# A hybrid streaming encoder step with 32 experts: the half pass put last, the overflow loop two passes earlier, two weight units beside the ring, and the gate/up bias loaded within the first pass

## The chip, the cores and the metric

The kernel runs on one core of a Trainium2 chip. The metric is the device time of one execution in microseconds. The profiler's span is the time from the first to the last instruction of the profiled execution; it is a little shorter than the execution's own time.

## The reference, cut to what matters

The layer has a mixer (one wide projection, a gated recurrent branch, a spatial gating branch, an output projection), and behind it a mixture of experts. There are 384 tokens (256 of a prompt, 8 x 16 of running streams), a model width of 1024, 32 experts and 4 experts for each token. All is float32.

```python
x = x + mixer(rms_norm(x, norm1_g), ...)
h = rms_norm(x, norm2_g)
logits = h @ w_router + b_router
gates = softmax(top_k(logits, 4))
for e in range(32):
    gate, up = split(h[tokens_of(e)] @ w_gate_up[e] + b_gate_up[e])    # 1024 -> 2 x 1024
    gate, up = minimum(gate, 7), clip(up, -7, 7)
    act = (up + 1) * gate * sigmoid(1.702 * gate)
    x[tokens_of(e)] += gates_of(e) * (act @ w_down[e] + b_down[e])
y = rms_norm(x, final_norm_g)
```

The weights of one expert are 12 MB (8 MB gate/up, 4 MB down), so the 32 experts bring 384 MB through the DMA.

## The kernel before, in words

**Engines.** The kernel is written with one instruction stream for each engine and semaphores between them. SP (SyncE) issues nearly all loads, in one order written out by hand. POOL (GpSimd) issues a few small loads and prepares for each pass the matrix `pick`, which gathers tokens, and `sel`, which selects bias rows. TensorE (PE) multiplies, ACT and DVE (ScalarE and VectorE) read PSUM.

**The mixer** comes first (to about 294 us of the span). Its weights pass through a small ring of their own (`raw`), are split into a high and a low part by ACT and DVE (L571, L784), and are multiplied at L1208 to L1210. While it runs, places in SBUF come free one after the other, and SP loads the first units of expert weights into them (`load_expert`, L335 to L337 and its calls up to L377).

**Passes.** The experts are ranked by their number of tokens, and 17 passes (`UNITS`, L70) take them in turn. A pair pass takes two experts, each with 64 of the 128 token slots (the two wide passes split 96 and 32). One solo pass (pass 8) gives all slots to one expert. The half pass takes one expert with 64 tokens and puts the two halves of the output columns side by side, so it needs half the matmuls. Before, the order is: passes 0 to 7 pairs and wide pairs, pass 8 solo, 9 to 13 pairs, pass 14 the half pass, 15 and 16 pairs. Passes are counted from 0 here, so "the fifteenth" is pass 14.

**Within a pass** (`experts_pass`, L1503) TensorE does, for k = 0 to 7, the gate/up product of 128 rows of the weights (L1537); behind k=0 it adds the bias by a matmul with `sel` (L1552; the half pass has L1549 and L1550); behind k=1 and k=3 it combines the output of the pass before into PSUM for the three token tiles (L1470, L1471; in pass 0 it is the down bias, L1477), and DVE adds these to y (L1132). Then come the gather of the tokens of the next pass (L1453), the turning of the activations (L1500), for which DVE and ACT have made gate and up (L1146 to L1150, L722), and the down product (L1591). The output is scaled by ACT (L738, in the last pass L735).

**The ring.** Expert weights stand in 16 places of 1 MB (`RING_AT`, `wexp`), and two places together take 2 MB in one load from pass 1 on (L391). One unit is 1 MB; a pair pass needs 24, a solo or half pass 12. The load of unit n waits until TensorE has used unit n - 16 (`wexp_used`). In front of the last pass stands the overflow loop: if an expert had more tokens than its slots, passes are added at run time, in up to three groups of eight. With these inputs no group is taken, but every engine steps over the loop. The first 12 units of the pass behind it wait for unit n - 12, since their places are those which the loop would use.

**Behind the last pass** TensorE combines (L1617, L1618), DVE adds (L1190), ACT squares (L762), DVE and ACT make the roots (L1194 to L1196, L765), and the final gain is applied to token tiles 0 and 2 by DVE (L1200) and to tile 1 by POOL and ACT (L561, L768). SP stores three tiles of 512 KB (L416).

**Bias and gain.** `bias_raw` (0.5 MB) is loaded by POOL in the mixer (L479) and split into its high and low part by DVE at L971 and L972; `fnb`, the final gain in all partitions (0.5 MB written), is loaded by POOL at L475.

Of the kernel before, what the change touches and what calls it, by code (L numbers as in the profile page):

```python
# [34 lines left out]
P = 128  # L35
# [40 lines left out]
OVER_SLOTS = tuple((LOADS[LAST] + m_) % RINGS for m_ in range(EXP_U))  # L76
OVER_ROWS = 5
OVER_GROUP = 8
# [22 lines left out]
def hawk_gmlp_moe_streaming_step(  # L101
# [6 lines left out]
    with ExitStack() as ctx:  # L108
# [4 lines left out]
        def sem(name):  # L113
# [57 lines left out]
        bias_raw = at("bias_raw", 176128, [2 * NE, 2 * D])  # L171
# [5 lines left out]
        fnb = at("fnb", 205824, [P, D])  # L177
# [26 lines left out]
        mask = at("mask", 112128, [P, TT, NE], BF16)  # L204
        iota_p = at("iota_p", 98432, [P, P])
        gat_t = at("gat_t", 201728, [3 * NE, T], F32R)
        gat3 = at("gat3", 203264, [P, TT, 3, NE])
        cnt = at("cnt", 204416, [P, NE])
        key = at("key", 204544, [P, NE])
        rank = at("rank", 204672, [P, NE])  # L210
        cap = at("cap", 204928, [P, 3, NE])
        order_f = at("order_f", 204800, [1, NE])
# [6 lines left out]
        squares = at("squares", 201728, [P, D])  # L219
        y_gain = at("y_gain", 131072, [P, D])  # L220
# [13 lines left out]
        fnb_loaded, n2p_loaded = sem("fnb_loaded"), sem("n2p_loaded")  # L234
# [29 lines left out]
        gat_ready = sem("gat_ready")  # L264
# [16 lines left out]
        sq3, gained, r3_in, r3_out, out_final, stored = (  # L281
            sem("sq3"), sem("gained"), sem("r3_in"), sem("r3_out"), [sem(f"out_final{t}") for t in range(TT)], sem("stored"))
# [45 lines left out]
        def _(sp):  # L328
# [28 lines left out]
            sp.wait_ge(mrg_ready, CB)  # L357
            load_expert(4)
# [20 lines left out]
            for n in range(RINGS, 2 * EXP_U):  # L379
                sp.wait_ge(wexp_used, n - RINGS + 1)  # L380
                sp.dma_start(wexp[n % RINGS][:], exp_one(n % 2, n // 2)).then_inc(exp_landed[n % RINGS], 16)
            sp.wait_ge(order_ready, 1)
            def load_pass(unit, later, ids, ring, last=False):

                for n in range(0, EXP_U * len(ids), 2):
                    m, x, slot = n // 2 // len(ids), n // 2 % len(ids), (unit + n) % RINGS
# [9 lines left out]

            for it in range(1, LAST):
                load_pass(LOADS[it], 0, ranked(it), lambda n: RINGS)
            sp.wait_ge(table_ready, 1)
            groups_on = sp.value_load(cnt_i[0:1, 0:1], min_val=0, max_val=OVER_GROUPS)  # L400
            with sp.Fori(0, OVER_GROUPS) as a:
                with sp.If(a < groups_on):
                    for b in range(OVER_GROUP):
                        e = sp.value_load(over_e[0:1, bass.ds(a * OVER_GROUP + b, 1)], min_val=0, max_val=NE - 1)
                        load_pass(LOADS[LAST], a * (OVER_GROUP * EXP_U) + b * EXP_U, [e], lambda n: EXP_U)
                sp.nop()
            ids = ranked(LAST)
            load_pass(LOADS[LAST], groups_on * (OVER_GROUP * EXP_U), ids, lambda n: EXP_U if n < EXP_U else RINGS, True)
            for k in range(2):
                for x in range(2):  # L410
                    sp.dma_start(wexp[(LOADS[NU] - 3 + 2 * x) % RINGS][:, D * k:D * k + D],
                                 exp_two(ids[x], EXP_U // 2 - 1)[:, D * (2 + k):D * (3 + k)]).then_inc(last_landed[k][x], 16)
            for t, dst in ((0, y_prompt[:, 0:P, :].rearrange("o p d -> (o p) d")), (1, y_prompt[:, P:2 * P, :].rearrange("o p d -> (o p) d")),
                           (2, y_sample.rearrange("b s d -> (b s) d"))):
# [1232 lines left out]
```

## Time and profile before

| | us |
|---|---|
| median of 3 runs | 1244.13 (1243.86 to 1244.79) |
| the profiled execution's own time | 1245.88 |
| its span | 1243.8 |
| TensorE busy | 1181.9 |
| DVE busy | 396.3 |
| ACT busy | 226.7 |
| POOL busy | 82.4 |

The mean granted clock of TensorE is 0.988 of full speed. The DMA moved 443.67 MB in the span. In a window's row the columns are the stretch, its length, busy time and number of instructions of each engine, the granted clock of TensorE as a share of full speed, the busy share of the DMA engines, and GB/s. In a row of the timeline or of the chain the first number is the start in us from the span's start and the second the time in us.

### The profile page before, as it was taken

The numbers are of one execution on the slowest core, as the hardware profiler recorded it, in microseconds if no ns is written. First come the engines' busy times: TensorE is split into PE (matmuls) and PEld (weight loads), VectorE is DVE, ScalarE is ACT, GpSimd is POOL, SyncE is SP. The second block draws the span as 40 slices with busy tenths as digits, with TensorE's granted clock in tenths as the row PEclk, the third lists the DMA queues.
The fourth block names the chain that finished last, engine by engine and source line by source line (L and its number), as shares of the span: only waits on it lengthen the run. The fifth ranks groups of instructions, "written<-read, shape, count | busy, mean of one in ns | idle before, by whom it ended". The sixth has DMA issues, their size and how long they took to land.

```text
span 1243.8 us, 15675 instructions
## 1 busy us (share of the span) xinstructions
PE 1181.9 (95%) x6447; PEld 675.1 (54%) x6447; DVE 396.3 (32%) x649; ACT 226.7 (18%) x389; POOL 82.4 (7%) x243
## 2 busy tenths in 40 slices
PE   7999999999999999989999999999999898999896
PEld 6999999985435354343434343544435353544332
DVE  4648586756242313131211111221211121212023
ACT  4533672223101011010101010100101010110112
POOL 4100000010201010000100010101101010110000
PEclk9999999999999999999999999999999999999898
DMA  6553227578999999999999999899999999999992
GB/s 226 155 166 107 98 86 256 194 291 341 419 428 427 427 428 428 426 426 427 427 428 427 429 426 427 353 385 421 427 428 428 428 427 427 427 428 428 425 422 95
DMA packets 48828, 443.67 MB, mean 357 GB/s; under 512 B 4620, under 2 KB 4716, under 8 KB 22576
## 3 DMA queue, kind: packets, MB, share of 16 engines
q1 hardware_dynamic: 47488, 439.43, 85.6%
q0 software_dynamic: 1264, 3.20, 1.0%
q8 instruction: 51, 0.84, 0.3%
q14 instruction: 25, 0.20, 0.0%
HBM read 440.63 MB, written 1.98 MB: 356 GB/s over the span
## 4 chain that ended last, share of the span: by engine, by line
PE 75%; DMA 21%; issue 1%; DVE 1%; ACT 1%; SPq 1%; DVEq 0%; ACTq 0%
PE ps L1537 24%; DMA wexp<-in_w_gate_up_dram 20%; PE ps L1591 17%; PE ps L1208 7%; PE ps L1453 7%; PE ps L1209 7%; PE ps L1210 7%; PE ps L1470 1%; PE ps L1500 1%; PE ps L1471 1%; PE ps L1308 1%; PE ps L1552 1%; PE ps L1462 1%; DMA raw<-in_w_in_dram 1%; PE ps L1422 0%
## 5 line engine op out<-in xcount | busy, mean ns | idle before, releaser
L1537 PE MATMUL ps<-wexp,xt 128*64 128x512 f32 (+1 forms) x2368 | 479.1, 606 | 34.4 <-DMA wexp<-in_w_gate_up_dram 28.8
L1537 PEld LDWEIGHTS ps<-wexp,xt 128*64 128x64 f32 (+1 forms) x2368 | 155.0, 133 | 328.9 <-issue 328.4
L1591 PE MATMUL ps<-wexp,act_t 128*64 128x512 f32 (+1 forms) x1184 | 232.0, 596 | 4.8 <-issue 4.0
L1591 PEld LDWEIGHTS ps<-wexp,act_t 128*64 128x64 f32 (+1 forms) x1184 | 88.3, 132 | 135.2 <-issue 134.1
L1132 DVE TENSOR_TENSOR y<-y,ps 128x1024 f32<-128x1024 f32 x51 | 60.7, 1218 | 216.9 <-PE ps L1471 214.8
L722 ACT ACTIVATE g<-g 128x512 f32<-128x512 f32 x33 | 20.8, 630 | 567.9 <-DVE g L1146 567.9
L1208 PE MATMUL ps<-act_h,split 128*128 128x384 f32 x352 | 118.0, 335 | 0.0
L1210 PE MATMUL ps<-act_h,split 128*128 128x384 f32 x352 | 117.6, 334 | 0.0
L1209 PE MATMUL ps<-act_l,split 128*128 128x384 f32 x352 | 117.6, 334 | 0.0
L1453 PEld LDWEIGHTS ps<-pick,xn 128*128 128x128 f32 x768 | 86.9, 192 | 13.0 <-issue 13.0
L1170 DVE SCALAR_TENSOR_TENSOR out_l<-ps,gate_now,out_h 128x1024 fp32r<-128x1024 f32 x16 | 20.5, 1283 | 225.4 <-ACT out_h L738 225.4
L1453 PE MATMUL ps<-pick,xn 128*128 128x128 f32 x768 | 90.0, 277 | 0.0
L784 DVE TENSOR_TENSOR split<-raw,split 128x2048 fp32r<-128x2048 f32 x29 | 66.2, 2290 | 69.7 <-ACT split L571 69.6
L1146 DVE TENSOR_SCALAR g<-ps 128x512 f32<-128x512 f32 x33 | 22.7, 687 | 194.7 <-PE ps L1537 194.7
L571 ACT ACTIVATE split<-raw 128x2048 fp32r<-128x2048 f32 x30 | 57.6, 1919 | 95.5 <-PE ps L1210 69.0
L1208 PEld LDWEIGHTS ps<-act_h,split 128*128 128x128 f32 x352 | 66.1, 188 | 0.6 <-issue 0.4
L1209 PEld LDWEIGHTS ps<-act_l,split 128*128 128x128 f32 x352 | 66.1, 188 | 0.1
L1210 PEld LDWEIGHTS ps<-act_h,split 128*128 128x128 f32 x352 | 66.1, 188 | 0.0
L738 ACT ACTIVATE out_h<-ps,gate_now 128x1024 fp32r<-128x1024 f32 x16 | 17.8, 1113 | 212.2 <-PE ps L1591 212.2
L1470 PE MATMUL ps<-out_h,pick_tg 128*128 128x512 f32 x96 | 41.3, 430 | 0.0
L715 ACT ACTIVATE xt<-ps,small 128x128 f32<-128x128 f32 x128 | 36.4, 371 | 18.6 <-PE ps L1453 18.6
L499 POOL TENSOR_SCALAR pick<-iota_p,pos_e 128x64 f32<-128x64 f32 (+2 forms) x93 | 39.2, 445 | 3.3 <-POOL pos_e L512 2.9
(304 smaller groups left out, 814.9 us busy)
## 6 DMA issues: line engine op xcount, KB each, us to landing
wexp<-in_w_gate_up_dram SPq DMA_DIRECT2D x120, 2048.0 KB, 24.0
wexp<-in_w_down_dram SPq DMA_DIRECT2D x58, 2048.0 KB, 25.4
raw<-in_w_in_dram SPq DMA_DIRECT2D x20, 1024.0 KB, 5.1
wexp<-in_w_gate_up_dram SPq DMA_DIRECT2D x16, 1024.0 KB, 8.6
wexp<-in_w_down_dram SPq DMA_DIRECT2D x10, 1024.0 KB, 8.2
raw<-in_w_proj_a_dram SPq DMA_DIRECT2D x4, 1024.0 KB, 5.7
raw<-in_w_out_dram SPq DMA_DIRECT2D x4, 1024.0 KB, 5.0
raw<-in_w_proj_b_dram SPq DMA_DIRECT2D x2, 1024.0 KB, 6.8
```

Source lines behind the costliest of these rows:

```text
L499: i_ = pool.tensor_scalar(pick[:, t, s0:s0 + width], iota_p[:, 0:width], pos_e[:, t, x:x + 1], None, ALU.is_equal)
L571: act.activation(split_h[:, n % MIX_SPLIT], raw[:, n % MIX_RING], ACT.Copy).then_inc(high_done, 1)
L715: i_ = act.activation(xt[:, 4 * k + c, :], ps[:, 4 + k, c * P:(c + 1) * P], ACT.Copy, scale=n2p[:, 4 * k + c:4 * k + c + 1])
L784: dve.tensor_tensor(split_l[:, n % MIX_SPLIT], raw[:, n % MIX_RING], split_h[:, n % MIX_SPLIT].bitcast(F32), ALU.subtract).then_inc(low_do ...
L1132: dve.tensor_tensor(y[:, t, :], y[:, t, :], ps[:, b:b + 2, :].rearrange("p a b -> p (a b)"), ALU.add).then_inc(y_added, 1)
L1208: pe.matmul(out, a_h, b_h, start=start, stop=False)
L1209: pe.matmul(out, a_h, b_l, start=False, stop=False)
L1210: return pe.matmul(out, a_l, b_h, start=False, stop=stop)
L1453: i_ = pe.matmul(ps[:, 4 + c // 4, c % 4 * P:(c % 4 + 1) * P], xn2[:, t, c * P:(c + 1) * P], pick[:, t], start=t == 0, stop=t == TT - 1)
L1470: pe.matmul(o, pick_tg[:, t * P:(t + 1) * P], out_h[:, UC * k:UC * k + UC], start=True, stop=False)
L1537: i_ = pe.matmul(ps[s0:s0 + w, b, :], xt[:, k, s0:s0 + w], wexp[place(k, x)][:, at_:at_ + UC], start=k == 0, stop=k == CB - 1)
L1591: i_ = pe.matmul(ps[s0:s0 + w, 6 + c, :], act_, wexp[place(CB + m, x)][:, D * kk + UC * c:D * kk + UC * c + UC], start=k == 0, stop=k == C ...
```

## The change

- The half pass moves from place 14 to the end; passes 9 to 15 are seven pair passes. In the last pass there is no gather for a next one.
- The overflow loop stands in front of pass 14 (`OVER_AT`), on all engines. Passes 14, 15 and 16 follow it, with their waits counted from a register value.
- Units 0 and 1 (k=0 of the two experts of pass 0) get places of their own, `wfirst`: one in the place of the recurrent branch's weights, loaded by SP within the mixer, one in the place of the low part of the mixer's activations, loaded in front of `load_expert(4)`. The ring's first 16 units are now 2 to 17. A unit still waits for unit n - 16.
- `bias_raw` is loaded by POOL when k=0 of pass 0 is done, into the place of `wfirst[0]`; DVE splits it behind the ranking, in front of its first additions to y; TensorE adds the bias of pass 0 behind k=5 instead of k=0.
- `fnb` is loaded by POOL behind its preparation of pass 2.
- Behind the last pass the token tiles are taken in another order, DVE applies the gain to all three, POOL and ACT to none, and the last tile is stored in two halves.
- Several small tables lie elsewhere in SBUF.

```diff
-         + [((SOLO_RANK,), SOLO)] + [(r, PAIR) for r in PAIR_RANKS[5:10]] + [((HALF_RANK,), HALF)] + [(r, PAIR) for r in PAIR_RANKS[10:12]])
+         + [((SOLO_RANK,), SOLO)] + [(r, PAIR) for r in PAIR_RANKS[5:12]] + [((HALF_RANK,), HALF)])
+OVER_AT = LAST - 2
+PLACES = [n_ - 2 for n_ in LOADS]
+LAST_ORDER = ((0, 0), (1, 0), (0, 1), (1, 1), (2, 0), (2, 1))
...
+        wfirst = [at("wfirst0", 201728, [P, 2 * D]), at("wfirst1", 114688, [P, 2 * D])]
...
             def load_expert(n):
-                sp.dma_start(wexp[n][:], exp_one(n % 2, n // 2)).then_inc(exp_landed[n], 16)
+                u = n + 2
+                sp.dma_start(wexp[n][:], exp_one(u % 2, u // 2)).then_inc(exp_landed[n], 16)
...
+                if n == PB_U + 1:
+                    sp.wait_ge(gates_mm, 4)
+                    sp.dma_start(wfirst[0][:], exp_one(0, 0)).then_inc(first_landed[0], 16)
...
             sp.wait_ge(mrg_ready, CB)
+            sp.dma_start(wfirst[1][:], exp_one(1, 0)).then_inc(first_landed[1], 16)
             load_expert(4)
...
-            for n in range(RINGS, 2 * EXP_U):
-                sp.wait_ge(wexp_used, n - RINGS + 1)
+            for n in range(RINGS, 2 * EXP_U - 2):
+                u = n + 2
+                sp.wait_ge(wexp_used, u - RINGS + 1)
...
-            load_pass(LOADS[LAST], groups_on * (OVER_GROUP * EXP_U), ids, lambda n: EXP_U if n < EXP_U else RINGS, True)
+            load_pass(LOADS[OVER_AT], later, ranked(OVER_AT), lambda n: EXP_U if n < EXP_U else RINGS)
+            for it in range(OVER_AT + 1, LAST):
+                load_pass(LOADS[it], later, ranked(it), lambda n: RINGS)
+            load_pass(LOADS[LAST], later, ids, lambda n: RINGS, True)
...
-            pool.wait_ge(gates_mm, 4)
-            pool.dma_start(fnb[:], final_norm_g...).then_inc(fnb_loaded, 16)
-            pool.wait_ge(unit_used, PA_U)
-            for k in range(2):
-                pool.dma_start(bias_raw[k * NE:(k + 1) * NE, :], ...).then_inc(bias_loaded, 16)
...
+            pool.wait_ge(wexp_used, 2)
+            for k in range(2):
+                pool.dma_start(bias_raw[k * NE:(k + 1) * NE, :], ...).then_inc(bias_loaded, 16)
             pool.wait_ge(order_ready, 1)
-            for it in range(1, LAST):
+            for it in range(1, OVER_AT):
                 prepare(it, it)
+                if it == 2:
+                    pool.wait_ge(combined, TT)
+                    pool.dma_start(fnb[:], final_norm_g...).then_inc(fnb_loaded, 16)
...
-            pool.tensor_tensor(y_gain[:], y[:, 1, :], fnb[:], ALU.mult).then_inc(gained, 1)
...
             dve.tensor_copy(order_i[:], order_f[:]).then_inc(order_ready, 1)
+            dve.wait_ge(bias_loaded, 32)
+            link(dve.tensor_copy(bias_hl[:], bias_raw[:]))
+            dve.tensor_tensor(bias_hl[NE:2 * NE, :], ..., ALU.subtract).then_inc(bias_ready, 1)
...
+            last_stats(slice(0, 2), 4)
             dve.wait_ge(fnb_loaded, 16)
+            gain(0, slice(0, D), 1)
+            last_stats(slice(2, 3), 6)
+            gain(1, slice(0, D), 1)
+            for c in range(2):
+                gain(2, slice(UC * c, UC * c + UC), 2)
...
-                    if k == 0:
+                    if k == (5 if first else 0):
+                        if first:
+                            pe.wait_ge(bias_ready, 1)
                         pe.wait_ge(sel_ready, it + 1)
...
-            experts_pass(groups_on * OVER_GROUP + LAST, LOADS[LAST], groups_on * OVER_GROUP, ..., False, True)
+            for it in range(OVER_AT, NU):
+                experts_pass(groups_on * OVER_GROUP + it, PLACES[it], groups_on * OVER_GROUP, ..., False, it == LAST)
```

## Rows read from the trace of the kernel before

**Rows 1.** The page, part 2: GB/s in 40 equal slices of the span.
```profile
GB/s 226 155 166 107 98 86 256 194 291 341 419 428 427 427 428 428 426 426 427 427 428 427 429 426 427 353 385 421 427 428 428 428 427 427 427 428 428 425 422 95
```

**Rows 2.** The waits, whole span: us in total, times, longest us.
```profile
PE ps L1537 <- DMA wexp<-in_w_gate_up_dram: 28.8, 16, 3.1
...
PE ps L1537 <- issue: 5.3, 1, 5.3
```

**Rows 3.** The chain of work that ended last, in order of time.
```profile
718.12 8.79 PE ps L1537 x32
...
734.25 13.95 PE ps L1591 x64
748.21 3.43 PE ps L1537 x16
...
801.74 3.43 PE ps L1537 x16
...
1050.75 7.09 PE ps L1537 x32
...
1139.78 7.10 PE ps L1537 x32
...
1173.42 6.64 PE ps L1537 x16
```

**Rows 4.** Windows: end of the mixer, and the start of pass 16.
```profile
272.00:281.00 9.00, 9.00 (x49) 6.57 (x47) 1.87 (x5) 2.62 (x7) 0.00 (x0) 1.00 0.04 15
...
1173.40:1180.00 6.60, 6.58 (x17) 1.90 (x17) 0.00 (x0) 0.00 (x0) 0.00 (x0) 0.54 1.01 423
```

**Rows 5.** Timeline of the half pass (pass 14), then of pass 16 and the output.
```profile
1078.93 1.92 PE L1537 MATMUL ps<-wexp,xt 128*64 128x512 f32 x8
...
1097.57 5.62 PE L1453 MATMUL ps<-pick,xn 128*128 128x128 f32 x48
...
1104.60 7.03 PE L1591 MATMUL ps<-wexp,act_t 128*64 128x512 f32 x32
...
1194.90 13.95 PE L1537 MATMUL ps<-wexp,xt 128*64 128x512 f32 x64
...
1213.02 15.65 PE L1591 MATMUL ps<-wexp,act_t 128*64 128x512 f32 x64 [0.83 <-ACT act_t L728]
1227.92 1.48 ACT L735 ACTIVATE out_h<-ps,gate_now 128x512 fp32r<-128x512 f32 x2 [15.41 <-PE ps L1591]
...
1234.35 1.67 DVE L1194 TENSOR_TENSOR small<-small 128x2 f32<-128x2 f32 x1 [0.26 <-ACT squares L762]
...
1236.78 2.48 DVE L1200 SCALAR_TENSOR_TENSOR y<-y,small,fnb 128x1024 f32<-128x1024 f32 x2
```

**Rows 6.** DMA of unit 15, issued by SP (L337) at 286.9 us.
```profile
DMA to landing us min/median/max: 14.5/14.5/14.5
```

**Rows 7.** DMA of unit 18, issued by SP (L381) at 304.1 us.
```profile
DMA to landing us min/median/max: 5.0/5.0/5.0
```

**Rows 8.** Timeline of pass 0: bias, down bias, first additions to y.
```profile
298.19 1.19 PE L1552 MATMUL ps<-bias_hl,sel 64*128 64x512 f32 x4
...
308.59 2.35 DVE L1132 TENSOR_TENSOR y<-y,ps 128x1024 f32<-128x1024 f32 x2
...
312.17 0.73 PE L1477 MATMUL ps<-bdn_hl,gat_t 96*128 96x512 f32 x2
```

**Rows 9.** The tile bias_raw: its conversion on DVE, its loads by POOL.
```profile
L971 DVE CAST bias_hl<-bias_raw x1: 1214/1214/1214, 259.5 to 259.5; 64x2048 fp32r<-64x2048 f32 x1
L972 DVE TENSOR_TENSOR bias_hl<-bias_raw,bias_hl x1: 2281/2281/2281, 260.8 to 260.8; 32x2048 fp32r<-32x2048 f32 x1
...
DMA to landing us min/median/max: 4.8/5.2/5.5
```

**Rows 10.** DMA of unit 32, issued by SP (L391) at 338.0 us.
```profile
DMA to landing us min/median/max: 10.1/10.1/10.1
```

**Rows 11.** Window at the end of the stores.
```profile
1242.50:1243.00 0.50, 0.00 (x0) 0.00 (x0) 0.00 (x0) 0.00 (x0) 0.00 (x0) 0.50 0.67 254
```

More of the change, by code:

```diff
@@ L746, in _ @@
             act.preload_act_table(ACT.Silu)
-            for it in range(LAST):
-                experts_pass(it, LOADS[it], len(UNITS[it][0]), False, UNITS[it][1] is HALF)
+            for it in range(OVER_AT):
+                experts_pass(it, LOADS[it], len(UNITS[it][0]), False)
             act.wait_ge(table_ready, 1)
@@ L761, in _ @@
                     act.wait_ge(sq3, n - 1)
-                act.activation(squares3[:, n % 2], y[:, t, UC * c:UC * c + UC], ACT.Square, accum_out=rt[:, 32 + n:33 + n]).then_inc(sq3, 1)
-            for ts in (slice(0, 2), slice(2, 3)):
-                act.wait_ge(r3_in, 1 if ts.start == 0 else 2)
-                act.activation(rt[:, 40 + ts.start:40 + ts.stop], rt[:, 44 + ts.start:44 + ts.stop], ACT.Sqrt).then_inc(r3_out, 1)
-            act.wait_ge(gained, 1)
-            act.wait_ge(r3_out, 1)
-            act.activation(y_gain[:], y_gain[:], ACT.Copy, scale=rt[:, 41:42]).then_inc(out_final[1], 1)
+                act.activation(squares3[:, n % 2], y[:, t, UC * c:UC * c + UC], ACT.Square,
+                               accum_out=rt[:, 32 + TT * c + t:33 + TT * c + t]).then_inc(sq3, 1)
+                if n == 4:
+                    act.wait_ge(r3_in, 1)
+                    act.activation(rt[:, 40:42], rt[:, 44:46], ACT.Sqrt).then_inc(r3_out, 1)
+            act.wait_ge(r3_in, 2)
+            act.activation(rt[:, 42:43], rt[:, 46:47], ACT.Sqrt).then_inc(r3_out, 1)
         @block.vector
@@ L1513, in landed @@
                     for x in range(experts):
[L1514 removed]
+                        if first and k == 0:
+                            pe.wait_ge(first_landed[x], 16)
+                            continue
+                        slot, turn_ = place(k, x), (unit + 2 * (experts * (k // 2) + x)) // RINGS + 1
                         if first:
[L1516 to L1518 removed]
+                            turn_ = (experts * k + x - 2) // RINGS + 1
                         pe.wait_ge(exp_landed[slot], later * 16 + 16 * turn_ if later is not None and slot in OVER_SLOTS else 16 * turn_)
@@ L1536, in experts_pass @@
                             at_ = UC * (b + n) if half else UC * b
-                            i_ = pe.matmul(ps[s0:s0 + w, b, :], xt[:, k, s0:s0 + w],
-                                           wexp[place(k, x)][:, at_:at_ + UC], start=k == 0, stop=k == CB - 1)
+                            weights = wfirst[x] if first and k == 0 else wexp[place(k, x)]
+                            i_ = pe.matmul(ps[s0:s0 + w, b, :], xt[:, k, s0:s0 + w], weights[:, at_:at_ + UC], start=k == 0, stop=k == CB - 1)
                             if k == CB - 1 and b == 2 and (n == 0 if half else n == len(strips(shape)) - 1):
@@ L1553, in experts_pass @@
                         i_.then_inc(sel_used, 1)
-                        if first:
-                            token_gates(0, 7)
-                            pe.wait_ge(gat3_ready, 1)
-                            for t in range(TT):
-                                i_ = pe.transpose(ps[0:3 * NE, 6, t * P:(t + 1) * P], gat3[:, t].rearrange("p k e -> p (k e)"), ident[:])
-                            i_.then_inc(post_mm, 1)
+                    if first and k == 0:
+                        token_gates(0, 7)
+                        pe.wait_ge(gat3_ready, 1)
+                        for t in range(TT):
+                            i_ = pe.transpose(ps[0:3 * NE, 6, t * P:(t + 1) * P], gat3[:, t].rearrange("p k e -> p (k e)"), ident[:])
+                        i_.then_inc(post_mm, 1)
                     if k == 1:
```

140 lines of the change are left out of this document (68 added, 72 removed).

## The prediction

> **What bounds the kernel now.** I read the page's slices first. From the twelfth slice to the last but one the DMA moves 421 to 429 GB/s, but for two slices after pass 8 (353 and 385) [rows 1], so the expert passes run on a saturated stream of weights, while TensorE is busy too. The waits say how the two share the bound: TensorE waited for gate/up weights 16 times, 28.8 us in all and never over 3.1 us [rows 2]. I call the six steps of a pass A (k=0,1), B (k=2,3), C (k=4,5), D (k=6,7), E and F (the two halves of the down product). The longest waits stand before D. In the chain [rows 3] pass 8 begins at 748.21 and pass 9 at 801.74: 53.53 us for a pass without a wait. From D of pass 13 (1050.75) to D of pass 15 (1139.78) the stream brought 12 + 24 = 36 units of 1 MB in 89.03 us, 2.473 us each; a pair pass has 24, so 59.4 us. A pair pass is therefore DMA-bound by 5.8 us, once the lead of the 16-place ring is used up.
>
> But the end is not DMA-bound. After D of pass 15 no wait for a DMA stands in the chain. TensorE's next work after pass 15 begins at 1173.42 [rows 3], behind 5.26 us of standing still with "issue" as the cause [rows 2]; so pass 15 ended at 1168.16, 28.38 us after its D began. The 5.26 lie where the skipped overflow loop is, and the next stretch runs at a granted clock of 0.54 [rows 4]: 16 matmul records took 6.64 us [rows 3], where they take 3.43 to 3.65 elsewhere (801.74). The last 0.75 us before the down product's end already belongs to the output stage, which begins with ACT at 1227.92 [rows 5].
>
> **Half pass last, overflow loop at pass 14.** The new order has D13 where it was (same loads before it), and then two pair passes and the half pass.
> - The loop's cost moves to the head of pass 14: start 1078.9 + 5.26 = 1084.2 [rows 2, 5]. From A to D the present last pass needed 1173.42 to 1194.90 + 7.0 = 28.5 us, slow clock included. TensorE is at D14 at 1112.7; its weights land at 1050.75 + 59.4 = 1110.1. So the loop's price is absorbed here except 2.6 us, and no wait is left.
> - D14 to the next A is 28.4, A to D 53.53 - 28.38 = 25.2: TensorE is at D15 at 1166.3. Its weights land at 1050.75 + 48 x 2.473 = 1169.5. So TensorE waits 3.2 us, and D15 starts at 1169.5, against 1139.78 now: 29.7 later.
> - After D15 all six loads of the half pass come in time: its last weights land 20 units later, at 1219.0, while its down product starts only after 1220. To the half pass 28.4 (1197.9). Its gate/up part takes 1078.93 to 1097.57 = 18.6 [rows 5], so 1216.5. Then the activation chain, with nothing of TensorE's beside it: 4.17 now (1208.85 to 1213.02) when the first bank's part overlaps, 7.03 in today's half pass with the gather in between (1097.57 to 1104.60) [rows 5]. I take 4.3, near the lower end, because the half pass needs one activation chain and no gather; it is 4.2 to 5. Down product 7.03, plus 1.70, because after this kind of gap it took 15.65 now [rows 5] against 13.95 elsewhere [rows 3]. End of the down product 1229.5, against 1228.67 now. The ACT read of the first half starts 0.75 before the end now; in the half pass both halves end together, so some 0.2 before: 1229.3 against 1227.9. **Term: +1.4.**
>
> **Two units beside the ring.** The wait for unit n is the same before and after (n - 15 used); only units 16 and 17 profit, loaded before instead of at 298.3. The DMA was idle from 272 to 281 [rows 4], but those loads come into it only as shifted places: the queue now holds units 14 to 17 until 286.9 + 14.5 = 301.4 [rows 6], and unit 18 still waits for k=1. That was issued at 304.1 and landed in 5.0 [rows 7]; it can be issued 1.1 earlier, because four bias matmuls leave k=0 [rows 8]. So the 4.9 us of two units don't leave the stream; 1.1 does. **Term: -1.1**; bounds -4.9 (the units leave the stream in full) and 0.
>
> **Bias within pass 0, fnb in pass 2.** The four bias matmuls only move from k=0 to k=5. The conversion on DVE (1.21 + 2.28 [rows 9]) moved from the mixer, where TensorE was busy through it, in front of the first additions to y. The first two additions begin at 308.59 and take 2.35 [rows 8]; 1.1 earlier, at 307.5, the conversion now begins, it ends at 311.0, and the first addition (1.2) ends at 312.2 instead of 309.8. Behind it TensorE wants the third down-bias tile at 312.17 - 1.1 = 311.1: it stalls 1.2. Does that starve the stream? The tightest load of pass 0, unit 32, is issued at 338.0 and lands 10.1 later [rows 10]; into an idle queue a 2 MB load would need 5.0 + 2.45 = 7.4. Of the spare 2.7, 1.2 + 1.1 go; 0.4 is left. Cost 0, hidden by the queue. The bias load itself (0.5 MB) falls into the idle place from 301 on. POOL's wait for k=0 holds up only its prepare(1), which waits for order_ready anyway. fnb (0.5 MB) now goes through a full stream: 0.52 MB / 428 = **+1.2** (0 to 2.4). In the mixer the two early loads of SP take 2.45 us of DMA each and hold up what is queued behind them by so much (a load of proj_a; the router's and b_down's weights). TensorE is not seen waiting for any of these loads (the waits name only gate/up weights) and the queue runs empty at 272 [rows 4]. Cost 0 (0 to 0.5), covered by the buffers of the mixer.
>
> **Output stage.** DVE's first statistics took 1.67 us beside POOL's y_gain product [rows 5], for two elements a partition, so nearly all of it is waiting. That goes, but DVE takes tile 1 over from POOL and ACT, 1.2 as for one of the two tiles in 2.48 [rows 5], so its last product still ends some 11.3 us after the first ACT read. What changes is the stores: now tiles of 1.5 MB in all leave from 1238.1 on, and the last bytes move after 1242.5 [rows 11], 3.7 us at 428 GB/s: they stand in a queue. Tile 0 will leave 1.7 us earlier and the last store is 256 KB behind an almost empty queue. **Term: -0.9** (0 to -1.3). The Trainium skill (DMA: Bandwidth & Descriptors, Anatomy of one DMA) gives a DMA 2.0 us plus its bytes at 436 GB/s, by which halving the last store would give 0.6, an estimate; no run here shows a single store alone.
>
> **Sum:** 1.4 - 1.1 + 1.2 - 0.9 = +0.6 us. The profiled execution took 1245.88 (span 1243.8 and 2.1 around it), 1.75 over the median of 1244.13, and is the one that the sum is made against; on the median it gives 1244.7. A measurement here tells 0.2%, 2.5 us, from no change. That is the forecast: the removed stall and the shorter pass are worth no more than the 12 units by which D15 comes later.
>
> **The rivals.**
> - *Slower by the clock.* Of seven waits of 2.7 to 3.1 us before D, four were followed by a step of 8.5 to 8.8 us instead of 7.1; one of each kind stands in the chain, 718.12 (8.79) and 1139.78 (7.10) [rows 3]. D15's wait of 3.2 is now on the path that sets the end: nothing behind it absorbs 1.7 us. And the gap of 4.3 before the down product could cost like the one of 5.26, 3.2 instead of 1.7. One of them gives 1244.7 + 1.7 = 1246.4, both 1247.9. It decides if the granted clock falls behind D15. 0.27.
> - *Slower by a late bias.* Chance 0.08. If the bias lands after DVE's ranking chain (307.5), everything in DVE behind its wait is late, y_added too, and TensorE's stall at k=3 empties the stream. Issued only at 307.5 it would land 5.2 later, at 312.7 [rows 9], be converted at 316.2, added at 317.4: TensorE 6.3 late, of which 1.5 is in the spare and stall above, so 4.8 of the stream: 1249.5. Against it: DVE is idle at 298.4, when POOL issues. The Trainium skill (SBUF — State Buffer, SBUF: two separate sides) says that POOL cannot write the descriptors of its own DMA while DVE runs a two-port operation, which speaks for this rival, and by it the time would be 1249.5; no row here shows a POOL load issued beside that chain.
> - *Faster by the preload.* If the stream is shortened by both units (for that its queue would have to be busy beyond 303), the whole schedule up to D7 and after moves 4.9 instead of 1.1: 1240.9. Against it: the landing at 301.4. 0.15.
> - *The loop does not stall in its new place*, or more: within 3.2 us of slack before D15, nothing changes. 0.05, same time.
>
> **Numbers.** Forecast 0.45. Faster by over 0.2%: the preload rival and a little of the forecast, 0.17. Slower: most of the clock rival with its upper part, the late bias: 0.26. Same 0.57. The range reaches from 1241.3 (part of the preload) to 1247.9 (both clock losses).
>
> **What would show it.** Right: D15 begins near 1169.5 of the span after a wait of about 3 us, the issue stall of some 5 us stands before pass 14, the down product of the half pass begins near 1221, DMA idle around 302 to 305. Wrong: no wait before D15 (then TensorE, not the stream, bounds passes 14 and 15), no DMA gap after 301, waits of TensorE on the bias in pass 0, a granted clock below 1 behind D15.

## The result, and the profile after

The changed kernel took 1247.64 us (median of 9 runs, 1245.24 to 1251.16) against 1244.79 for the kernel before (9 runs); the ratio is 1.0026 with a 95% interval of 1.0015 to 1.0036. So it is slower, by 0.15 to 0.36%. The profiled execution took 1247.42 us with a span of 1245.7; before it was 1245.88 and 1243.8.

The slices of the page (GB/s), to be held against [rows 1]:

```profile
GB/s 226 154 167 108 96 69 278 191 320 303 408 424 428 429 426 427 426 427 427 428 427 428 427 427 428 361 402 416 429 428 428 427 426 428 425 428 428 426 421 73
```

From the twelfth slice on the stream is as full as it was. What the change did to it before that is too short for slices of 31 us; the windows further down show it. The waits (us in total, times, longest) answer to [rows 2]:

```profile
PE ps L1565 <- DMA wexp<-in_w_gate_up_dram: 28.9, 16, 3.1
...
PE ps L1565 <- issue: 5.0, 1, 5.0
```

In sum nothing has changed here, so the sum doesn't tell where the time went. The chain of work that ended last, in order of time (start, duration), answers to [rows 3]:

```profile
719.81 7.09 PE ps L1565 x32
734.24 13.95 PE ps L1620 x64
748.20 3.43 PE ps L1565 x16
...
991.34 8.55 PE ps L1565 x32
...
1050.55 7.10 PE ps L1565 x32
1080.85 3.06 issue
1083.91 6.61 PE ps L1565 x16
...
1169.07 8.43 PE ps L1565 x32
1184.86 13.95 PE ps L1620 x64
```

D of pass 7 (D7) begins 1.7 us later than before (718.12), but takes 7.09 instead of 8.79, so pass 8 begins at the same time in both. D of pass 13 (D13) too stands where it stood. The standing still (issue) is now in front of pass 14, and D of pass 15 begins at 1169.07 and takes 8.43. Windows of the same trace (us; busy time of PE, PEld, DVE, ACT, POOL with the number of instructions; then the granted clock, the DMA share, GB/s), the first against [rows 4]:

```profile
272.00:281.00 9.00, 9.00 (x49) 6.67 (x47) 1.88 (x5) 2.62 (x7) 0.00 (x0) 1.00 0.35 145
302.00:304.00 2.00, 2.00 (x10) 0.81 (x6) 1.93 (x3) 0.00 (x0) 0.00 (x0) 1.00 0.02 4
1083.90:1090.52 6.62, 6.61 (x17) 1.99 (x17) 0.00 (x0) 0.00 (x0) 0.00 (x0) 0.55 1.02 426
1169.07:1177.50 8.43, 8.43 (x33) 2.83 (x33) 1.50 (x3) 0.63 (x1) 0.00 (x0) 0.84 1.01 430
1221.99:1231.24 9.25, 9.25 (x34) 2.62 (x30) 0.00 (x0) 0.00 (x0) 0.00 (x0) 0.76 0.00 0
```

The early units fill a third of the hole of the mixer (145 GB/s, 15 before). In exchange the queue runs empty at 302 (4 GB/s), where it moved 418 before: a new hole, as the prediction expected. The last three windows have a granted clock below 1: for part of each, TensorE ran at 1.2 GHz instead of 2.4. Two of them, D15 and the last down product, lie where nothing behind them absorbs a loss. The timeline of the end answers to [rows 5]:

```profile
1219.75 1.13 PE L1526 MATMUL ps<-ident,u 128*128 128x128 f32 x4 [2.44 <-DVE u L1165]
...
1221.99 9.25 PE L1620 MATMUL ps<-wexp,act_t 128*64 128x512 f32 x32
1231.34 1.27 ACT L749 ACTIVATE out_h<-ps,gate_now 128x512 fp32r<-128x512 f32 x2 [9.82 <-PE ps L1620]
...
1237.44 0.15 DVE L1208 TENSOR_TENSOR small<-small 128x2 f32<-128x2 f32 x1
...
1240.00 2.59 DVE L1215 SCALAR_TENSOR_TENSOR y<-y,small,fnb 128x1024 f32<-128x1024 f32 x3
...
1241.95 0.99 SPq L431 DMA_DIRECT2D out_dram<-y  x2
```

ACT's first read of the last down product starts at 1231.34, 3.4 us later than before, and from there the kernel needs 14.4 us to its end (1245.7) where it needed 15.9. Pass 0, against [rows 8, 9]:

```profile
298.67 1.00 POOL L554 DMA_DIRECT2D bias_raw<-in_b_gate_up_dram  x2 [2.46 <-PE ps L1565]
...
307.46 1.21 DVE L1099 CAST bias_hl<-bias_raw 64x2048 fp32r<-64x2048 f32 x1
308.70 2.28 DVE L1100 TENSOR_TENSOR bias_hl<-bias_raw,bias_hl 32x2048 fp32r<-32x2048 f32 x1
...
311.01 3.48 DVE L1147 TENSOR_TENSOR y<-y,ps 128x1024 f32<-128x1024 f32 x3
...
312.38 0.70 PE L1503 MATMUL ps<-bdn_hl,gat_t 96*128 96x512 f32 x2 [1.16 <-DVE y L1147]
```

That is the forecast almost to the tenth: conversion at 307.5, first addition done at about 312.2, TensorE stalled by 1.16. But the stream shows the stall later. The same three microseconds before and after:

```profile
339.00:342.00 3.00, 3.00 (x18) 1.21 (x16) 0.00 (x0) 0.00 (x0) 0.00 (x0) 1.00 1.02 415
...
339.00:342.00 3.00, 3.00 (x16) 1.21 (x14) 0.00 (x0) 0.00 (x0) 0.00 (x0) 1.00 0.81 262
```

Here the stream moved 262 GB/s instead of 415, which at 428 GB/s is 1.1 us lost. The load that was due, unit 32, was issued at 339.4 instead of 338.0 [rows 10], because TensorE began the down product of pass 0 at 335.58 instead of 334.13, and 1.16 of these 1.45 us are the stall for the bias. The bias landed 3.8 to 4.2 us after its issue. D of passes 3 to 7 begins 1.3 to 1.7 us later than before (482.27, 542.08, 601.23, 660.06 and 719.81 against 480.97, 540.40, 599.65, 658.38 and 718.12).

So in the profiled executions the span grew by 1.9: +3.6 between D13 and ACT's read, -0.2 up to D13, -1.5 behind the read. The medians differ by 2.85: the execution profiled before was slow for its kernel (1245.88 against medians of 1244.1 to 1244.8), with its clock low in D7.

### The profile page after: what moved, and what is told of

It is laid out like the page before. It is cut to its first block, busy times and chain, and to the rows that moved or that the text cites. A ratio compares the mean times of both kernels' runs of the same rounds, so it can differ in the third digit from the quotient of the medians.

```text
span 1245.7 us, 15713 instructions
## 1 busy us (share of the span) xinstructions
PE 1181.9 (95%) x6447; PEld 675.1 (54%) x6447; DVE 396.3 (32%) x651; ACT 226.1 (18%) x388; POOL 82.1 (7%) x242
## 4 chain that ended last, share of the span: by engine, by line
PE 75%; DMA 21%; DVE 2%; issue 1%; SPq 1%; ACT 0%; DVEq 0%; ACTq 0%
PE ps L1565 24%; DMA wexp<-in_w_gate_up_dram 20%; PE ps L1620 18%; PE ps L1234 7%; PE ps L1479 7%; PE ps L1235 7%; PE ps L1236 7%; PE ps L1526 1%; PE ps L1496 1%; PE ps L1497 1%; PE ps L1334 1%; PE ps L1581 1%; PE ps L1488 1%; DMA raw<-in_w_in_dram 1%; PE ps L1448 0%
```

## The experiments

A measure that all traces share is the time from the start of D13 to ACT's first read of the last down product ("the read"): **177.2** before, **180.8** after. The times are ratios to runs of the kernel before on the same chip.

### 1. The order and the loop's place alone

Kernel before, with these two edits:

```diff
-         + ... [(r, PAIR) for r in PAIR_RANKS[5:10]] + [((HALF_RANK,), HALF)] + [(r, PAIR) for r in PAIR_RANKS[10:12]])
+         + ... [(r, PAIR) for r in PAIR_RANKS[5:12]] + [((HALF_RANK,), HALF)])
+OVER_AT = LAST - 2      # the loop's pass, in all engines' programs
```

> The kernel before with the half pass last and the overflow loop in front of pass 14, nothing else of the change. My theory now (the order is at fault: D15 comes 29.5 us later, the half pass is only that much shorter less about 1.4 us, and the granted clock falls in the gap before the last down product): D15 at about 1169.5 of the span, the first ACT read of the last down product at about 1231, span about 1246 to 1247.5, 2 to 3.5 us slower than before. Rival (the preload, the bias and the gain load in the stream are at fault, the order costs nothing): within 0.5 us of before.

Measured: ratio 1.0022 (1.0007 to 1.0037), 1246.72 us. The chain has:

```profile
1168.40 8.78 PE ps L1547 x32
...
1221.78 9.35 PE ps L1601 x32
```

D13 to the read: 181.1. D15 and the down product are slow as in the changed kernel, with nothing of its other parts there. The order with the loop costs 2.7 us by the ratio (2.4 by the medians) and 3.9 in the trace. The ratio's interval, 0.9 to 4.6 us, still holds the 1.4 of the forecast; the two traces, 3.9 here and 3.6 in the changed kernel, don't.

### 2. The loop in front of pass 14, old order

Kernel before with `OVER_AT = LAST - 2` alone.

> The kernel before with its own order (half pass at place 14) and only the overflow loop moved in front of pass 14. Theory: the loop's 5.3 us and the slow clock behind it (3 us) fall where later waits for weights absorb them: TensorE comes to D15 about 5 us late without a wait, to D16 at about 1199, just when its weights land; the down product then ends about 2.8 us earlier than before: span about 1241, 2 to 3.5 us faster. Rival (the loop was hidden already in its old place, since the stream sets the end): no difference.

Measured: ratio 0.9986 (0.9977 to 0.9996), 1242.44 us, a gain of 1.7 (0.5 to 2.9), where 2 to 3.5 was expected. Against the first run this is the price of the order alone: 1.0022 / 0.9986 = 1.0036, 4.5 us. Behind the loop the clock is low for long (window columns as above):

```profile
1083.08:1093.30 10.22, 10.22 (x24) 3.55 (x25) 0.00 (x0) 0.00 (x0) 0.41 (x2) 0.54 1.01 423
```

and TensorE waits for no weights behind D13 any more; D13 to the read: 176.7.

### 3. The output stage alone

Kernel before with the new output stage: tile by tile instead of half by half, no product on POOL, the last tile stored in two halves.

> The kernel before with only the new output stage (other order of the tiles, gain on DVE alone, last tile stored in two halves). Theory: from the first ACT read of the last down product to the end of the span 14.4 us instead of 15.9, so 1.5 us faster, all of it in the stores. Rival (the gain on DVE alone is as long as it saves): 0 to 0.5 us.

Measured: ratio 0.9982 (0.9972 to 0.9992), 1241.76 us. The timeline of its end:

```profile
1222.49 1.48 ACT L735 ACTIVATE out_h<-ps,gate_now 128x512 fp32r<-128x512 f32 x2 [15.16 <-PE ps L1600]
...
1228.59 0.15 DVE L1191 TENSOR_TENSOR small<-small 128x2 f32<-128x2 f32 x1
...
1233.10 0.99 SPq L419 DMA_DIRECT2D out_dram<-y  x2
```

From the read to the end of the span (1236.9) it takes 14.4 us, as in the changed kernel, against 15.9 before: 1.5 us from the trace, 1.0 to 3.5 by the interval. The statistics fell from 1.67 us [rows 5] to 0.15 once POOL's product was gone; before, that product ran from 1233.65 for 2.35 us, and the statistics, begun at 1234.35, ended with it at 1236.0. That agrees with the Trainium skill (SBUF — State Buffer, SBUF: two separate sides), by which a VectorE operation with two SBUF inputs and a GpSimd operation take turns on one pair of ports and the later one stands still for the whole of the other.

### 4. The changed kernel in the old order

```diff
-         + ... [(r, PAIR) for r in PAIR_RANKS[5:12]] + [((HALF_RANK,), HALF)])
+         + ... [(r, PAIR) for r in PAIR_RANKS[5:10]] + [((HALF_RANK,), HALF)] + [(r, PAIR) for r in PAIR_RANKS[10:12]])
```

> The changed kernel with only the order put back (half pass at place 14, loop in front of it as changed). It keeps the preload, the late bias, the gain load in pass 2 and the new output stage. Theory: the order is what costs, so this is faster than before: -2.8 for the loop, -1.5 for the output stage, +1.7 at most for the stream: 1241 to 1242.7 of the span, some 4 to 5 us faster than the changed kernel. The D steps of passes 4 to 7 begin 1.3 to 1.7 us later than before, as in the changed kernel. Rival (the stream's loads are at fault): not faster than before.

Measured: ratio 0.9985 (0.9974 to 0.9995), 1242.54 us: the changed kernel without its order is faster than the kernel before, and the order costs 5.1 us here (1.0026 against 0.9985). The product of runs 2 and 3 is 0.9968; this run is 0.0017 above it. So the preload, the late bias and the load of the norm's gain cost about 2.1 us together; the intervals of the three runs leave some 1.5 us either way. D of passes 4 to 7 begins 0.7 to 1.0 us later than before, less than the 1.3 to 1.7 expected (run 8 has a steadier measure of this). The clock did not fall in its last down product (13.96 us for 64 matmuls).

### 5. The gap before the last down product filled

Changed kernel; the products go to a bank that nobody reads:

```diff
+                if last:
+                    for _ in range(10):
+                        pe.matmul(ps[:, 3, :], ones_b[:], zero_b[:], start=True, stop=True)
                 turn(it, 0, 2 if half else 1)
+                if last:
+                    for _ in range(3):
+                        pe.matmul(ps[:, 3, :], ones_b[:], zero_b[:], start=True, stop=True)
```

> The changed kernel with 13 more matmuls in the last pass only, whose results nobody reads: ten between the last gate/up product and the move of the gates, three behind it, in the 4.7 us in which TensorE has nothing to do before the half pass's down product (1217.3 to 1222.0). They take about 2.2 us at full clock and start no transfer. Theory 'clock': the down product takes 9.1 to 9.3 us instead of 7.0 because the granted clock falls behind the idle gap. Then with the gap filled it takes 7.0 to 7.2, its start stays at 1221.6 to 1222.2 (at most 0.3 later), and the time falls by 2.1 us: ratio to the kernel before about 1.001 instead of 1.0026. Rival 'the product is slow for another reason' (the order of its reads, or VectorE and ScalarE at the same PSUM banks): it still takes over 9 us, and the time stays or grows by 0.3. Between them: if the clock falls with the gap filled, the low stretch stands in the windows but not behind idle time.

Measured: ratio 0.9997 (0.9986 to 1.0008), 1245.03 us. The timeline:

```profile
1216.07 2.33 PE L1599 MATMUL ps<-zero_b,ones_b 128*128 128x512 bf16 x10
...
1218.58 0.75 PE L1526 MATMUL ps<-ident,u 128*128 128x128 f32 x4 [0.18 <-DVE u L1165]
1219.17 0.81 PE L1603 MATMUL ps<-zero_b,ones_b 128*128 128x512 bf16 x3
...
1220.26 7.03 PE L1626 MATMUL ps<-wexp,act_t 128*64 128x512 f32 x32
1227.39 1.27 ACT L749 ACTIVATE out_h<-ps,gate_now 128x512 fp32r<-128x512 f32 x2 [7.42 <-PE ps L1626]
```

More work on TensorE made the kernel faster. The down product takes 7.03 instead of 9.25, the transposes 0.75 instead of 1.13, and the gap (1216.07 to 1220.26) is 4.2 instead of 4.7. That is 2.7 us by the trace and 3.6 by the ratios, whose intervals leave room for either. In this trace D15 (1169.24) also took 7.09, after a wait of 1.6. The rival, that the product is slow for another reason, is out.

### 6. The loop back in front of the last pass

Changed kernel with `OVER_AT = LAST`.

> The changed kernel with its overflow loop moved back in front of the last pass (now the half pass) and nothing else. Theory of the prediction (the loop's 5 us of standing still and its stretch of low clock are absorbed in front of pass 14, where a wait for weights stands behind them): D of pass 14 and D of pass 15 each wait for weights again, D15 stays at 1168 to 1170, and the stall of 5.0 to 5.3 us and some 3 us of low clock come back whole on the path that sets the end: about +6.5 us over the changed kernel (it has up to 1 us of its own stretch covered by the loads), ratio to the kernel before 1.007 to 1.009. Rival 'the place of the loop is worth nothing with this order' (D15's wait takes it up anyway): within 1 us of the changed kernel, 1.002 to 1.004.

Measured: ratio 1.0064 (1.0040 to 1.0087), 1254.46 us (4 runs; the trace is of the slowest, 1258.75). Loss against the changed kernel: 4.7 us by ratio, 6.8 by median; the expectation was +6.5. D14 (1111.27) and D15 (1169.99) wait 2.7 us each, as this theory says, and the stall is back on the path:

```profile
1204.99 3.68 PE L1562 MATMUL ps<-wexp,xt 128*64 128x512 f32 x8 [5.04 <-issue]
```

The eight matmuls take twice the 1.92 of the same work elsewhere. D13 to the read: 191.6.

### 7. The loop's place and the output stage

Runs 2 and 3 together, on the kernel before.

> The kernel before in its own order of passes, with two parts of the change: the overflow loop in front of pass 14 and the new output stage. Alone they gave 1242.44 (0.9986) and 1241.76 (0.9982). Theory 'parts add' (one lies before the last pass, the other behind its down product): ratio 0.9968, 1240.4, no wait for weights after pass 13, the ACT read of the last down product near 1226 of the span and 14.4 us from there to the end. Rival 'the output stage's gain was a run whose clock fell less often': ratio 0.998, 1242. The forecast of the prediction for these two parts was -0.9 for the output stage and nothing for the loop's place, 0.9992.

Measured: ratio 0.9970 (0.9957 to 0.9982), 1241.28 us. The two parts add (0.9968 was expected). This beats both kernels. One line of its timeline was unexpected: `L1556` of D16 at 1198.52 behind a wait of 0.44 for weights. With little of the clock lost the last pass has reached the stream's pace (D13 + 148.3 us; 60 units at 2.473 are 148.4). The read came at 1222.96, 3 us before the 1226 expected, in an execution that was the fastest of this kernel but one.

### 8. The norm's gain loaded later

```diff
-                if it == 2:
+                if it == 10:
                     pool.wait_ge(combined, TT)
                     pool.dma_start(fnb[:], ...)
```

> The changed kernel with the load of the final norm's gain (0.5 MB) issued behind the tenth expert pass's preparation instead of the second's, so that it is transferred near 790 to 812 of the span, where the DMA engines had room in the kernel before. Theory 'the stream sets D15': from pass 3 to pass 7 the D steps begin 1.2 us earlier than in the changed kernel (481.1, 540.8, 600.0, 658.9, 718.6), but passes 8 and 9 begin where they did, since TensorE sets their start, and behind the solo pass the stream takes up again from the same place: the end moves by 0 to -1.2 us, ratio 1.0016 to 1.0026. Rival 'the load costs nothing': D steps where they were. If the D steps stay at +1.3 to +1.7 over the kernel before, the stream's loss lies in pass 0 and not in this load.

Measured: ratio 1.0004 (0.9990 to 1.0018), 1246.94 us. The chain:

```profile
718.39 8.54 PE ps L1565 x32
...
1050.57 7.10 PE ps L1565 x32
...
1168.84 8.59 PE ps L1565 x32
```

D of passes 4 to 7 begins at 540.65, 599.43, 658.21 and 718.39, 1.4 to 1.9 us earlier than in the changed kernel and within 0.3 of the kernel before. So the load's cost is real, and the preload's 1.1 had been lost by then. Single traces differ by as much as that, since pass 0 begins at different times in them (294.0 to 296.2). Counted in each trace from TensorE's first gate/up matmul, D7 stands at 424.9 to 425.1 us in the six traces with the changed pass 0 and the early gain load, at 423.9 in this run, and at 422.7 to 424.2 in the seven with the old loads. By this count the load costs 1.0 to 1.2 at D7, as forecast, and the preload has gained nothing. Pass 8 began where it did, as I expected, but not for my reason: D7 happened to run at the low clock here (8.54), see the next section. By the ratios the gain is 2.7 us, by the medians less (1.3); the intervals overlap at 1.0015 to 1.0018.

### 9. The loop in front of pass 12, new order

Changed kernel with `OVER_AT = LAST - 4`.

> The changed kernel with its overflow loop in front of pass 12 instead of pass 14, in a stretch where TensorE waits for weights in pass 12 (0.9 and 2.7 us) and pass 13 (1.2 and 2.7 us). Theory 'the stream sets D15' (the new order puts 12 units more ahead of it): D13 begins at 1049 to 1051 and D15 at 1168 to 1170 as before, the stall of 5 us only eats the waits in passes 12 to 14, and the time stays: ratio to the kernel before 1.002 to 1.003. Rival 'the loop in front of pass 14 is what the change costs' (its stall and the low clock behind it reach the end): with the loop earlier D15 begins 3 us or more earlier and the ratio is below 1.000. If the stall reaches the stream instead (places come free too late), D13 and D15 move later by 2 us or more.

Measured: ratio 1.0022 (1.0010 to 1.0035), 1247.64 us, the same as with the loop at 14, as the theory of the stream says. D13 begins at 1053.68 and D15 at 1171.14, still behind waits of 2.68 and 2.70. The absolute times are 2.7 and 1.1 us beyond my bounds for two reasons. Pass 0 began 1.5 us later in this execution (296.22 against 294.71), and D7 with it (721.12). And from the end of D7 to D13 it takes 325.5 us against 323.7 in the changed kernel, so 1.8 us of the stall of 5.4 did reach the stream: the third outcome of the expectation, in part.

### 10. The loop in front of pass 12, old order, new output stage

Run 7 with `OVER_AT = LAST - 4`.

> The kernel before in its own order, with the new output stage and the overflow loop in front of pass 12. In this order nothing waits for weights behind pass 15's D (D at 1136 to 1140), so the end is TensorE's, and the stall of 4.8 to 5.3 us with its 3 to 10 us of low clock costs in full wherever no wait follows: in front of pass 14 the two waits behind it took up some 1.7 us. In front of pass 12 four waits follow (0.9, 2.7, 1.2, 2.7 us) and then D15's. Theory 'a stall is taken up by as much waiting for weights as follows it': D13 stays at 1049 to 1051, D15 at 1136 to 1140 with its wait of about 2.8 us, and the end comes 5 us earlier than with the loop in front of pass 14: 1236 us, ratio 0.992 to 0.993. Rival 'late places': TensorE's delay holds back the stream, D13 moves later by 3 to 5 us, and the ratio is 0.996 to 0.997 as with the loop in front of pass 14.

Measured: ratio 0.9964 (0.9950 to 0.9978), 1240.38 us (6 runs). Neither theory gave this: D13 and D15 stayed where the first put them, but the time is that of the loop at 14. TensorE's timeline, at the end, shows where the gain went:

```profile
1138.73 7.09 PE L1556 MATMUL ps<-wexp,xt 128*64 128x512 f32 x32 [1.86 <-DMA wexp<-in_w_gate_up_dram]
...
1168.10 3.65 PE L1556 MATMUL ps<-wexp,xt 128*64 128x512 f32 x16 [0.98 <-DMA wexp<-in_w_gate_up_dram]
...
1188.41 7.09 PE L1556 MATMUL ps<-wexp,xt 128*64 128x512 f32 x32 [1.58 <-DMA wexp<-in_w_gate_up_dram]
1198.20 8.78 PE L1556 MATMUL ps<-wexp,xt 128*64 128x512 f32 x32 [2.70 <-DMA wexp<-in_w_gate_up_dram]
...
1211.14 13.95 PE L1610 MATMUL ps<-wexp,act_t 128*64 128x512 f32 x64 [0.83 <-ACT act_t L734]
```

TensorE arrives 5.6 us earlier at pass 16 than in run 7 (1167.1 against 1172.7) and waits 5.3 us there for weights: D16 is at the stream's pace, 59.5 us behind D15, and then the clock falls behind the wait. The old order's end is bounded by the stream at 1198.2 plus 24.4 us of TensorE at full clock.

### 11. The waits filled too

Run 5 and, ahead of the wait at D of passes 7 and 15:

```diff
+                    if k == 6 and shape is PAIR and unit in (PLACES[7], PLACES[15],):
+                        for _ in range(10):
+                            pe.matmul(ps[:, 0, :], ones_b[:], zero_b[:], start=False, stop=False)
                     if first or k % 2 == 0:
                         landed(k)
```

> The changed kernel with the gap before the last down product filled, as in the run with 13 more matmuls, and ten matmuls more that add zero to an accumulating bank, ahead of the wait for weights at D of pass 7 and at D of pass 15 (2.3 us of the 2.7 us that TensorE waits there). All traces so far agree that pass 12's D begins 264.0 to 264.6 us after the end of pass 7's D, and the end lies a fixed time behind the end of pass 15's D, so a fall of the clock in either step (8.4 to 8.8 us instead of 7.1) reaches the end. Theory 'clock': both steps take 7.1 us in every trace, and the time falls by another 1 to 2.5 us against the run with the gap alone (0.9997): ratio 0.998 to 0.999, with a narrower spread of times. Rival 'the fillers cost what they take' or do not hold the clock: ratio 0.9997 or above, steps still of 8.4 us or more in some trace.

Measured: ratio 0.9994 (0.9985 to 1.0004), 1243.53 us. Both steps took 7.09, and the wait behind the added matmuls was 0.43 to 0.44; the chain's D15:

```profile
1168.62 7.09 PE ps L1568 x32
```

But the time is 0.4 us from that of run 5, less than the intervals can tell, and its spread is no narrower. The part of the expectation that speaks of the time is not borne out; how often run 5's executions lose the clock at D15 is not known from its one trace.

### 12. Old order, loop at 12, waits filled

Run 10 with the same ten matmuls at D of passes 7 and 15.

> The kernel before in its own order, with the new output stage, the overflow loop in front of pass 12, and ten matmuls that add zero ahead of the waits at D of pass 7 and D of pass 15. Against the same kernel without the fillers: theory 'clock', both steps take 7.1 us, 1 to 2.5 us less, ratio 0.991 to 0.992 if the loop's stall is taken up in its new place, 0.995 if it isn't. Rival: no difference between the two.

Measured: ratio 0.9963 (0.9950 to 0.9975), 1240.37 us (8 runs): no difference from run 10, so the rival holds. D16 still waits 2.70 at 1196.70 and takes 8.67, and the last down product 15.65 instead of 13.95: the clock fell behind another wait, which I had left unfilled.

## Why the prediction was wrong

The forecast was 1244.7 and no change within 0.2%; measured on its base of 1244.13 it is 1.0026 x 1244.13 = 1247.4, slower, and just inside the range (1241.3 to 1247.9). I had given this outcome to the rival *slower by the clock*, at 0.27. Two things failed: steps behind idle time that the sum put at full clock or near it, and a stall in pass 0 that the sum put at nothing. That the rival's 1247.9 is so near is partly luck: the rival knew nothing of the 2 us that the stream lost, nor of the 1.3 that the output stage gained beyond its term, and these largely cancel. By its steps:

- **The stream to D15: right.** D13 stood (1050.55), D15 came at 1169.07 (1169.5 forecast), behind a wait of 2.7 (3.2); 118.3 to 119.0 us from D13 to D15 in six traces of the new order and 117.5 in run 9, for 48 x 2.473 = 118.7. The loop's stall in front of pass 14 was absorbed: 5.0 us, and D15 did not feel it.
- **"D15 at full clock": the first step that failed.** I took 7.10 for D15 from the one row of the trace that ended well, although by my own count four of seven such waits were followed by a slow step. It took 8.43. In the six traces of the new order where TensorE waited 2.6 to 2.7 us before D15 with nothing in the wait (the changed kernel, runs 1, 6, 8, 9) or 1.6 (run 5), the five long waits were all followed by 8.43 to 8.78 and the short one by 7.09. Up to the half pass this is +1.1 (29.54 against 28.4).
- **The gap before the down product: mis-sized.** Forecast 4.3 us and a product of 7.03 + 1.70; measured 4.68 and 9.25, and ACT's read 0.3 later within it than I took. That is +1.2. Run 5 shows that 2.7 us of this stretch is clock: filled, it is 4.2 and 7.03. With +0.1 for the gate/up part and -0.2 for the stream these make the 2.2 us by which D13-to-read (180.8) missed the forecast (178.55). The term was 1.4; the trace gives 3.6, run 1's ratio 2.7 (0.9 to 4.6).
- **What the order costs, whatever the clock does.** The old and the new order with the loop at 14 and a clean end are run 7 (172.7) and run 5 (176.7). In the old order the stream sets D16 (148.3 behind D13), and 24.4 us of TensorE follow; in the new one it sets D15 (118.6), and 58.1 follow. The half pass takes 29.7 us of stream out from in front of the last bound step and puts 33.7 us of TensorE behind it: 4.0 us. The sum had the change from before to after, loop and order together, and this does not make it wrong; but I had compared the new order only with a kernel that still paid for its loop, and so credited it with a gain (the stall absorbed) that the loop's place brings in either order.
- **Two units beside the ring, -1.1, and the late bias, 0: the second step that failed.** Unit 18 was issued 1.0 earlier (303.1) and landed 0.9 earlier (308.2 against 309.1), as forecast. Counted from TensorE's first gate/up matmul, unit 30 landed after 46.8 to 47.5 us in six of the seven traces with the changed pass 0 (48.4 in the changed kernel's own) against 47.7 to 48.6 in the seven with the old one, so most of them had the lead of about 1 us. Unit 34 landed after 58.3 to 58.8 against 57.6 to 58.9: the lead was gone. Between the two lies the hole at 339: 186 to 306 GB/s from 339 to 342 in the seven traces with the changed pass 0, 339 to 415 in the others. My line "into an idle queue a 2 MB load would need 7.4", and with it the 2.7 us to spare, was wrong: unit 32 took 9.1 us from issue to landing in the changed kernel and 7.9 to 9.2 in the seven traces, though the stream had already thinned. TensorE's stall of 1.16, booked at nothing, is most of the 1.4 us by which unit 32 was issued later, and there the lead was lost. The preload without the late bias was not run, so what each is worth alone is open.
- **The norm's gain in pass 2, +1.2: right.** 1.4 to 1.9 at the D steps against the changed kernel's trace, 1.0 to 1.2 at D7 counted from pass 0 (run 8).
- **Bias: the stall was forecast right** (1.2, measured 1.16), its cost was not (above). The rival of the late bias did not happen: it landed in 3.8 to 4.2 us, before the ranking chain ended.
- **How a delay in the passes before 8 reaches the end.** In eleven traces whose loop is not in front of pass 12, D12 begins 264.0 to 264.7 us behind the *end* of D7 (whether that end is late by its start or by its clock), and D13 58.7 to 59.5 behind D12, although D12 was slow (8.50 to 8.78) in every one. So TensorE carries D7's end through passes 8 to 11, while a slow D12 is absorbed. The profiled pair hid the loss of the stream: D7 began 1.7 later, but happened to run at full clock. In run 8 it was the other way round, 718.39 and 8.54, and the end was the same as in the changed kernel (read at 1231.35 and 1231.34).
- **Output stage, -0.9 (0 to -1.3): right in sign, too small.** 1.5 in the traces, 1.0 to 3.5 by run 3. DVE's last product ends 11.25 us behind the read as forecast (11.3); from there to the end of the span it takes 3.1 us instead of 4.5. I had taken only part of the queue of stores off.

The parts as measured: order +4.5 to 5.1, loop's place -1.7, output stage -2.2, preload with late bias and gain load +2.1. Their sum is +2.7 to 3.3, and the whole is +3.2 by ratio. The forecast of +0.6 was off by +1.3 (run 1's ratio) to +2.2 (the trace) in the term of order and loop, most of it the clock behind D15 and around the gap; by +2 in the stream; and by -1.3 in the output stage. Each of these parts is uncertain by 1 to 2 us.

The better kernel is the one before with the loop earlier and the new output stage: 0.9970 with the loop in front of pass 14, 0.9964 in front of pass 12, which are not told apart.

## What to carry to other kernels

When a kernel is bound by its stream, cost an order of work by two numbers: when the stream delivers what the last bound step needs, and how much engine time is left behind it; a small last unit helps only if it takes less engine time behind than stream time in front. A stall is absorbed as far as waits follow it before the next bound (in run 9 not quite: 1.8 of 5.4 us reached the stream), and moving it earlier than that gained nothing here, because the stream is next. A stall on TensorE can cost the stream even where no engine waits for a load yet: in pass 0 it made a load late, and the stream lost about 1 us behind it. Price a wait on TensorE's path with the slower step behind it, or fill it with work that nobody reads: that paid in run 5, and could not be told from nothing in runs 11 and 12.

## What the runs showed of the hardware

- **Waits of 2.7 us cost the clock, some of them every time.** TensorE waited 2.70 to 2.73 us before D12 in eleven traces, and each time D12 ran part of its 32 matmuls at the lower level (8.50 to 8.78 us instead of 7.1); before D7, with the same 2.70, five of the twelve unfilled traces kept 7.09, and before D13, with 2.68 to 2.84, seven of twelve. Ten filler matmuls, which leave at most 0.46 us of the wait, kept D7 and D15 at 7.09 in both traces that had them. The Trainium skill (TensorE: Matmul & The Clock Gate, HAM oscillation — how this bites in real kernels) tells of waits for a transfer that put the clock down again each time; the traces agree at D12 and, in the new order, at D15 (five of five behind 2.6 to 2.7 us), at 1.3 to 1.7 us a wait, but not at D7 and D13, where only a part of the waits did it.
- **A skipped loop costs twice.** The program's loop around an untaken branch stops TensorE for 4.8 to 5.4 us in all traces, and the matmuls behind it run at a granted clock of 0.54 to 0.55 for 6.6 us before and after, 10.0 in run 6 and 10.2 in run 2; in run 7 the first 7 us behind it had a mean of 0.79.
- **Executions of one kernel differ by 2 to 9.5 us** (1239.4 to 1241.4 in run 10, 1241.8 to 1251.3 in run 1). Where there are traces of the same passes, the falls of the clock land differently. A pair of traces can therefore hide a loss of 1.7 us, as it did here.
